# Moving each head's gate unit into the next head's pass, with the recurrence half a unit later, in a hybrid encoder layer on one core

## The reference, cut to what matters

```python
    z = u @ w_in                                   # 28 units of 128 columns: 7 kinds for each of 4 heads
    q = jax.nn.silu(heads(z[..., 0:W]))            # "q"
    v = heads(z[..., 3 * W:4 * W])                 # "v"
    f_logits = jnp.stack([heads(z[..., W:2 * W]), heads(z[..., 2 * W:3 * W])])   # "f" and "fb"
    ...
    o = gla_chunk_scan(qs, ks, vs, gs)             # the recurrence, forward and backward
    ...
    o = o * lax.rsqrt(jnp.mean(o * o, axis=-1, keepdims=True) + RMS_EPS)
    hg_out = o * hg_norm * jax.nn.silu(z[..., 4 * W:5 * W])                      # "g", the gate
    glu = z[..., 5 * W:5 * W + C] * jax.nn.sigmoid(z[..., 5 * W + C:5 * W + 2 * C])   # "a", "b"
    c = depthwise_conv(glu, conv_w, conv_b)        # 31 taps
    c = jax.nn.silu(layernorm(c, conv_ln_g, conv_ln_b))
    return jnp.concatenate([hg_out, c], axis=-1) @ w_out
```

## Time and profile before

| | us |
|---|---|
| median of three runs | 2799.11 |
| span of the profiled execution, first to last instruction | 2799.2 |
| PE busy (matmul) | 2635.1 (94%) |
| DVE busy | 1331.7 (48%) |
| ACT busy | 554.6 (20%) |
| granted TensorE clock, mean over the span | 0.974 |
| matmuls, L425 alone | 75% of the chain that ended last |

### The profile page before, as it was taken

One profiled execution on the slowest core, in us unless ns is written; L12 is line 12 of the kernel. 1 busy time (PEld: TensorE's weight loads), 2 busy tenths in 40 slices (PEclk: granted clock), 3 DMA queues, 4 the chain that ended last, 5 costly groups with the idle time before them and its releaser, 6 DMA issues.

```text
span 2799.2 us, 31878 instructions
## 1 busy us (share of the span) xinstructions
PE 2635.1 (94%) x13699; PEld 2232.0 (80%) x13699; DVE 1331.7 (48%) x1217; ACT 554.6 (20%) x599; POOL 23.1 (1%) x48
## 2 busy tenths in 40 slices
PE   7999999999999999898989779999999999999996
PEld 6888888888888878787878667788888888888884
DVE  4323343233432468877778775533333233333334
ACT  5111111111111132222322333311111111111114
POOL 0000000000000000000000000000000000000000
PEclk9999999999999999999999789999999999999998
DMA  4111111111111121010110201101111111111101
GB/s 130 38 38 39 38 38 35 35 39 38 38 39 31 57 80 46 21 45 26 31 33 33 97 29 57 43 31 38 38 39 38 39 38 38 39 38 31 38 23 75
DMA packets 146064, 119.92 MB, mean 43 GB/s; under 512 B 3841, under 2 KB 127937, under 8 KB 145921
## 3 DMA queue, kind: packets, MB, share of 16 engines
q1 hardware_dynamic: 141312, 98.64, 11.5%
q0 software_dynamic: 4608, 19.04, 1.7%
HBM read 103.18 MB, written 14.48 MB: 42 GB/s over the span
## 4 chain that ended last, share of the span: by engine, by line
PE 81%; DVE 10%; issue 4%; ACT 3%; DVEq 0%; DMA 0%; ACTq 0%; SPq 0%
PE PS L425 75%; DVE H L1214 2%; PE PS L599 2%; DVE T L1207 1%; DVE T L1205 1%; ACT WH L823 1%; DVE COUT L1440 1%; PE PS L604 1%; DVE BF L1329 0%; DVE BB L1329 0%; PE PS L631 0%; DVE AB L1327 0%; DVE WL L1111 0%; PE PS L729 0%; ACT Q L959 0%
## 5 line engine op out<-in xcount | busy, mean ns | idle before, releaser
L425 PE MATMUL PS<-XH,WH 128*128 128x512 f32 (+2 forms) x2976 | 763.0, 365 | 30.3 <-DVE XL L1172 12.1
L425 PE MATMUL PS<-XL,WH 128*128 128x512 f32 (+2 forms) x2976 | 750.2, 360 | 0.0
L425 PE MATMUL PS<-XH,WL 128*128 128x512 f32 (+2 forms) x2976 | 748.0, 360 | 0.0
L425 PEld LDWEIGHTS PS<-XH,WH 128*128 128x128 f32 x2976 | 499.0, 190 | 122.5 <-issue 27.4
L425 PEld LDWEIGHTS PS<-XL,WH 128*128 128x128 f32 x2976 | 500.4, 190 | 88.9
L425 PEld LDWEIGHTS PS<-XH,WL 128*128 128x128 f32 x2976 | 497.8, 190 | 88.1
L1214 DVE SCALAR_TENSOR_TENSOR H<-PS,H 128x1296 f32<-128x1296 f32 (+1 forms) x176 | 263.6, 1498 | 209.3 <-PE PS L425 209.3
L425 PE MATMUL PS<-HH,WH 128*128 128x512 f32 (+2 forms) x1056 | 269.1, 363 | 29.9 <-DVE H L1214 25.2
L1111 DVE TENSOR_TENSOR WL<-WR,WH 128x1024 fp32r<-128x1024 f32 (+1 forms) x171 | 205.6, 1203 | 185.4 <-ACT WH L823 185.3
L823 ACT ACTIVATE WH<-WR 128x1024 fp32r<-128x1024 f32 (+1 forms) x171 | 176.4, 1032 | 488.7 <-PE PS L425 474.7
L425 PE MATMUL PS<-HH,WL 128*128 128x512 f32 (+2 forms) x1056 | 264.6, 359 | 0.0
(11 more groups left out here) (210 smaller groups left out, 1272.4 us busy)
## 6 DMA issues: line engine op xcount, KB each, us to landing
WR<-in_ffn_w_gate SPq DMA_DIRECT2D x44, 512.0 KB, 3.7
WR<-in_ffn_w_up SPq DMA_DIRECT2D x44, 512.0 KB, 3.8
WR<-in_ffn_w_down SPq DMA_DIRECT2D x44, 512.0 KB, 3.5
WR<-in_w_in SPq DMA_DIRECT2D x28, 512.0 KB, 3.9
hsave<-H POOLq DMA_DIRECT2D x8, 648.0 KB, 3.2
XT<-in_x_sample SPq DMA_DIRECT2D x8, 512.0 KB, 10.6
out_sample<-XO SPq DMA_DIRECT2D x8, 512.0 KB, 5.4
H<-hsave POOLq DMA_DIRECT2D x5, 640.0 KB, 4.2
```

The lines of the kernel that those rows point to most:

```text
L425: mm = nc.tensor.matmul(SET[s][:, o:o + b - a], wt[:, wat[0], wat[1]:wat[1] + P], x(a, b), start=first and wt is WH and x is xh, stop=last ...
```

## The change

The units stand in a new order, g, a, b, v, q, f, fb, where g is that of the head before. Head 0 has six units; each pass has g of head i-1 and then a to fb of head i; a last g (head 3) stands ahead of the tail. Stage "v" and stage 0 of a head both run inside the g unit, and stage n in slot n+1 of the pass instead of slot n; the tail keeps stages 1 to 12 (slots 2 to 13). In stage 0 the raise stands after the first merge instead of after the third. The taps are dealt out anew: of the 31 of a head, 13 stood in the slots of stages 0 to 6, now 6.

```diff
-TAPS_BEFORE = {0: 2, 1: 2, 2: 1, 3: 2}
-TAPS_NOW = {4: 2, 5: 2, 6: 2, 7: 4, 8: 2, 9: 4, 10: 2, 11: 2, 12: 2, 13: 2}
+UNITS = ("g", "a", "b", "v", "q", "f", "fb")
+TAPS_BEFORE = {0: 3, 1: 1, 2: 1, 3: 1, 4: 1}
+TAPS_NOW = {6: 1, 7: 1, 8: 5, 9: 1, 10: 5, 11: 4, 12: 4, 13: 3}
...
-TAPS_LAST = {0: 2, 1: 3, 2: 2}
+TAPS_LAST = {0: 3, 1: 2, 2: 1, 3: 1}
...
+            def gate_and_start(i):
+
+                chunks_between, done = dense(0, i)
+                rec("v", i - 1, chunks_between)
+                chunks_between(4 - done[0])
+                rec(0, i - 1, chunks_between)
+                chunks_between(KD)
+
+            def head(i):
+
+                gate_and_start(i)
+                for pos in range(1, 7):
+                    chunks_between, done = dense(pos, i)
                     for half in range(2):
...
+                        chunks_between(PE_FIRST)
+                        rec(2 * pos + half - 1, i - 1, chunks_between)
+                        chunks_between(4 * half + 4 - done[0])
...
+            for pos in range(1, 7):
+                dense(pos, 0, 1)[0](KD)
...
             with looped(pe, 1, HEADS, head_counts(uses, tiles)) as i:
-                head(i, "z", True)
+                head(i)
+            gate_and_start(HEADS)
...
-            for slot in range(14):
+            for slot in range(2, 14):
...
-                rec(slot, HEADS - 1, chunks_between)
+                rec(slot - 1, HEADS - 1, chunks_between)
...
                 for pos in range(7):
...
+                    next_split(pos)
+                    rec(2 * pos - 1 if pos else "v", i - 1)
+                    rec(2 * pos, i - 1)
+                    unit_done(i, pos)
...
                 if stage in range(len(LEVELS)):
                     for n, (c0, c1) in enumerate(CHUNK_PIECES):
+                        if stage == 0 and n == 1:
+                            for later in (1, 2):
+                                piece(LEVELS[0], later)
+                            raise_level(0).then_inc(level_up, 1)
                         if n == 2:
                             taps_between(1)
...
-                    if not raise_first:
-                        if stage:
-                            dve.wait_ge(level_up, 7 * h + stage)
-                        else:
-                            dve.wait_ge(bks_ready, h + 1)
-                        raise_level(stage).then_inc(level_up, 1)
...
+            def head(i):
                 for slot in range(14):
...
+                    taps_between = (some_taps(i - 1, slot, TAPS_BEFORE, sum(TAPS_NOW.values())) if slot < 6 else
+                                    some_taps(i, slot, TAPS_NOW, 0))
+                    if slot % 2 == 0:
+                        next_split(slot // 2)
+                    rec(slot - 1 if slot else "v", i - 1, taps_between)
+                    if slot % 2:
+                        evacuate(i, UNITS[slot // 2], taps_between)
                     taps_between(TAPS)
+                dve.wait_ge(y_ready, i)
```

More of the change, by code:

```diff
@@ L721, in _, with dense, chunks_between @@
-            head(0, "first", False)
+            def dense(pos, i, first=None):
+                s, slot = pos % 2, HEAD_SLOTS[pos]
+                lo = 0 if UNITS[pos] in FULL_UNITS else META
+                unit(slot)
+                done = [0]
+                def chunks_between(n):
+                    for k in range(done[0], min(done[0] + n, KD)):
+                        if k == 0:
+                            claim(s)
+                        if first == pos:
+                            pe.wait_ge(xl_ready, KD + k + 1)
+                        if first == pos - 1 and k == 6:
+                            spread_r(1, 0)
+                        mm = product(s, (slot, k * P), lambda a, b: XH[:, k, a:b], lambda a, b: XL[:, k, a:b],
+                                     blocks(lo), k == 0, k == KD - 1)
+                        if k == KD - 1:
+                            mm.then_inc(t_full[s], 1)
+                    done[0] = min(done[0] + n, KD)
+                return chunks_between, done
@@ L1019, in _ @@
             act.wait_ge(h_saved, 16 * KD)
-            head(0, "first", False)
-            with looped(act, 1, HEADS, head_counts(uses, tiles)) as i:
-                head(i, "z", True)
+            for pos in range(1, 7):
+                next_split(pos)
+                if pos == 2:
+                    roots(1, 0)
+                unit_done(0, pos)
+            with looped(act, 1, HEADS, head_counts(uses, tiles)) as i:
+                head(i)
+            split(EARLY_SLOTS[0])
+            split(EARLY_SLOTS[1])
+            tiles[0].add()
+            rec("v", HEADS - 1)
+            rec(0, HEADS - 1)
+            unit_done(HEADS, 0)
             def hi_part(n, src):
@@ new lines, in next_split, with some_taps, taps_between @@
+            def next_split(pos):
+                split((HEAD_SLOTS + HEAD_SLOTS[0:1])[pos + 1])
+            def some_taps(i, slot, counts, j0):
+                left = [j0 + sum(counts[a] for a in counts if a < slot),
+                        j0 + sum(counts[a] for a in counts if a <= slot)]
+                def taps_between(n):
+                    for _ in range(min(n, left[1] - left[0])):
+                        tap(i, left[0])
+                        left[0] += 1
+                return taps_between
@@ L1508, in head @@
                     taps_between(TAPS)
+                dve.wait_ge(y_ready, i)
             dve.wait_ge(pad_set, 2)
-            head(0, "first", False)
+            for slot in range(2, 14):
+                taps_between = some_taps(0, slot, TAPS_NOW, 0)
+                if slot % 2 == 0:
+                    next_split(slot // 2)
+                elif slot == 3:
+                    mean_squares(1, 0)
+                else:
+                    if slot == 5:
+                        make_r(1, 0)
+                        evacuate(0, "a", taps_between)
+                    evacuate(0, UNITS[slot // 2], taps_between)
+                taps_between(TAPS)
```

232 lines of the change are left out of this document (81 added, 151 removed).

## The result

The changed kernel takes 2827.38 us (median of four runs, 2825.99 to 2831.36) where the kernel before takes 2799.24 (four runs): 1.0102 times as long, with a 95% interval of 1.0088 to 1.0117. It is slower by 28 us; the forecast was slower by 14, and the time lies 0.4 us above the range.

What follows compares the result with a forecast made beforehand. PE, busy 94% of the span, was taken as the bound, losing time only where it waits. Three passes of 162.4 us lose 17.9, the tail wins 4.0: 2799.2 + 17.9 - 4.0 = 2813.1 us, range 2797 to 2827.

Steps and rivals of the forecast that it cites:

- E: Start of fb's evacuation on DVE, from which stretches are measured; before the change at 1089.1, 1244.1, 1401.55 and 1558.4.
- Stage 6 to the next E: Last stretch of a pass, up to fb's next evacuation: 62.6 us, where it took 51.05 before.
- The sign: Whole kernel: slower than before, forecast 2813 us against 2799.2; slower had a chance of 0.64.
- piece 3 of stage 1: PE in each pass: this piece waits 5.5 us for DVE's merge, where before it waited for nothing.
- The third diagonal piece: PE behind fb's evacuation: DVE's row, taps included, frees this piece at E+18.0.
- The wait for ACT's copies: PE ahead of stage 1: the earlier wait of 4.33 us falls to under 1.
- The broadcast's wait: PE at the norm's broadcast, near a pass's end: waits 0.9 us for DVE to reach the norm's diagonal.
- E to stage 3 in the tail: Tail behind the last fb evacuation: 67.2 us instead of 71.1, 4.0 won.
- the 0.7 for low clock: From E to the end of stage 0: low clock adds 0.7 us, giving E+27.2 instead of E+26.5.
- Stages 2 to 6: Middle of a pass: 52.55 us becomes 51.2; waits of 1.58 and 2.54 stay, 1.35 goes.
- The low clock from E on: Rival: clock stays at 1.2 GHz through diagonal and stage 0, some 3.3 us a pass more, 2823 us; chance 0.16.
- The cover: Rival: gate unit fills PE's hole, DVE reaches stage 1's first merge in time; passes of 153.0, 2783.5 us; chance 0.16.

Runs made afterwards that it cites:

- the three taps moved: Changed kernel with the three taps between KS and the diagonal moved behind the diagonal: 2819.43 us, ratio 1.0069.
- g later: Changed kernel with g's evacuation behind stage 1's merges and GS ahead of stage 2's raise in the passes: 2820.61 us, ratio 1.0072.
- the kernel with all parts: Changed kernel with other PSUM sets, slot 0's three taps behind the diagonal, levels' raises first, splits behind stages, g's evacuation and GS later: 2778.74 us, ratio 0.9929.
- the raise first: Kernel before, with DVE's raise first in levels 1 to 6 and tap, split of slots 2, 4, 6 and GLU behind: 2787.65 us, ratio 0.9954.

## Why the prediction was right in direction and short in size

Two steps failed. The sum began at the first E, so head 0 was a term put at nothing: it cost 5.1. And "Stage 6 to the next E" was costed at full clock behind the sums of squares: the clock fell there in all three passes, 1.55 us each, most of the 5.4 by which the three passes together are longer than in the sum. 5.1 and 5.4, and 0.3 in the tail, are the 10.8 between 2813.1 and the profiled span of 2823.9.

**What held.** The sign, and the mechanism behind it: the waits on DVE's queue at the two places that the prediction named. It gave 5.5 us for piece 3 of stage 1; it was 5.16, 5.18 and 5.19. The third diagonal piece at E+18.0: 17.9, 18.0 and 18.0. The wait for ACT's copies under 1: 0.5. 1.52 and 2.56 kept, one stage later. The broadcast's wait 0.9: 1.0. E to stage 3 in the tail 67.2: 67.05, and the tail's gain 4.0: 3.7. The runs show each cause and not only its place: with the three taps moved the diagonal is free; with tap and split behind the raise half of the 5.18 goes, with g later the other half, and with both all of it.

**What was too small: a pass, 162.4 against 164.2.** Piece 3 of stage 1 was to start at E+45.7 and starts at E+45.0 in the second pass: the 0.7 for low clock up to the end of stage 0 did not come there (it did in the first, where the piece starts at E+46.5). For the low clock behind it I took 2.3; it cost 2.8 in the first pass and 1.4 to 1.5 in the others. The two steps behind it were short by the low clock alone. "Stages 2 to 6" were to take 51.2: behind the 2.56 at stage 5 two chunks took 5.3 instead of 3.8 in passes 2 and 3, where the prediction had read from the earlier trace rows that a wait of that size leaves no slowing. "Stage 6 to the next E" was 62.6 and measures 64.2 in the second pass: the eight chunks behind the sums of squares took 15.8 instead of 14.25, in all three passes. The prediction looked for low clock only behind waits, and the kernel before had none at this place (1.00 in the line of 1392.00). That the sum is right at the end of stage 6, E+99.8 against E+99.5 in the second pass, is luck: two terms were too large and one was missing. Its count of 23 taps in the last six slots is also wrong, by the tables it is 22; nothing in the sum hangs on it.

**What was missed: head 0, 5.1.** I started the sum at the first E and took it as fixed. Measured from the last wait of FFN 1 it is 6.2 later, and both causes are edits whose text I had read. The first unit of head 0 moved from an even to an odd place and so to the set that FFN 1 frees last: 4.2 up to the first evacuation, of which other sets win back 2.6, and all of it (41.1) in the kernel with all parts. The new table of taps, made for the passes, puts 22 of 24 taps into head 0's last six slots and makes DVE 2.0 late for fb. (FFN 1 up to its last wait was 1.1 shorter in this execution, so 6.2 show as 5.1.) "SP's new order of loads and POOL's stores cost nothing" stands, as in the mixing block from 1009 us on no wait of ACT or DVE is put down to a DMA, but it was the wrong part to look at; a change of places is also a change of buffers, and must be costed at the loop's entry as well as inside it.

**The rivals.** The low clock from E on gave 2823, near the result, but mostly not by what happened: the first 16 matmuls of the diagonal ran at full clock in all passes (1.95 us, as in the tail's pieces of the earlier trace rows). Behind the third piece the clock fell in the first pass only (0.58 from 1112 to 1116, 1.6 us); the other low clock came behind stage 1, stage 5 and the sums. The cover did not hold, for the reason given, DVE's 13.7 us against PE's 8.25. The Trainium skill ("Perfetto Trace Analysis", section "Optimization Strategy") says that interleaving two regimes may gain. As the change stands it loses 28 us; with DVE's queue set in order the same interleaving takes 2778.74, 22 under the kernel before. But the kernel before gains 12 from the raise first alone (2787.65), and its taps were not dealt anew, so what of the 22 the interleaving gives is not shown; against that kernel it is 9. So the runs bear the rule out at most where the second engine has room at the place that the work is put.

**Stayed open.** Why the clock falls behind the sums of squares in some passes and not in others, with the same instructions on PE; and the 3.4 us between the medians that the two profiles leave out.

## What to carry to other kernels

In a ring of engines, what stands ahead of the step that the others wait for is paid until another wait takes over (moving 2.8 us of tap and split won 2.6 of the 5.18; moving 5.0 us of taps brought the diagonal's end 2.3 forward, where PE's own work ends), and what stands behind it was mostly free here: put the ring's own step first in each stage, and evacuations, splits and filler work behind it, before deciding on a new order of the large units. When work moves by half a period, cost the loop's entry and exit too: which buffer the first unit takes, who frees that one last, and whether a table made for the steady state also fits the first round. And look for the next thing in the queue: a step that leaves it uncovers the wait behind it.
